# First modulation in four quarters of two feature tiles, x and ctx loaded first, key products placed beside the gate and value products

## What is computed

```python
sh_a, sc_a, g_a, sh_f, sc_f, g_f = jnp.split(
    (jax.nn.silu(c) @ w_ada[l] + b_ada[l])[:, None, :], 6, axis=-1)
...
hc = modulate(rmsnorm(ctx, norm_mix[l]), csh_a, csc_a)
hx = modulate(rmsnorm(x, norm_mix[l]), sh_a, sc_a)
...
u = h @ w_in
```

## Time and profile before

| | us |
|---|---|
| median of three runs | 1447.3 |
| the profiled run, device time | 1446.77 |
| its span, first to last instruction | 1444.9 |
| outside the span | 1.87 |
| PE busy in the span | 1395.9 (97%) |
| PE's waits for modulation chunks in the first 110 us | 14.9 |
| first product of `first_linear` | 31.30 |
| first product of ka | 46.95 |
| first product of qa | 52.46 |
| first scores of the attention | 75.40 |

### The profile page before, as it was taken

How to read it: one execution, slowest core, us unless ns; L and a number is a source line. 1 busy time by engine, 2 the same in 40 slices (tenths; PEclk the granted TensorE clock), 3 DMA queues, 4 the chain that set the end, 5 groups by cost and what they waited for, 6 DMA issues and landing times.

```text
span 1444.9 us, 21620 instructions
## 1 busy us (share of the span) xinstructions
PE 1395.9 (97%) x8272; PEld 1165.5 (81%) x8272; DVE 848.0 (59%) x1638; ACT 657.8 (46%) x1069; POOL 839.9 (58%) x672
## 2 busy tenths in 40 slices
PE   5999999999999999889999999999999999999998
PEld 3977798999988889547788888888888966888887
DVE  3798666786568798687664333321136667644422
ACT  3555755455553234783332222222226386545443
POOL 1534427999855444785254554544446630799997
PEclk9999999999999999999999999999999999999999
DMA  9748515777767753001355555533333320455664
GB/s 365 292 162 303 177 46 195 254 259 233 259 230 247 237 180 98 27 30 59 131 204 188 190 201 189 191 108 97 104 95 115 118 77 12 135 187 190 187 189 135
DMA packets 71207, 242.01 MB, mean 167 GB/s; under 512 B 7488, under 2 KB 12992, under 8 KB 70720
## 3 DMA queue, kind: packets, MB, share of 16 engines
q1 hardware_dynamic: 68688, 236.63, 49.2%
q10 hardware_dynamic: 2416, 4.00, 0.9%
HBM read 238.50 MB, written 1.05 MB: 166 GB/s over the span
## 4 chain that ended last, share of the span: by engine, by line
PE 51%; DVE 4%; ACT 2%; issue 1%; POOL 0%; DMA 0%; DVEq 0%; ACTq 0%
PE bank L762 9%; PE bank L768 9%; PE bank L763 9%; PE bank L623 8%; PE bank L624 4%; PE bank L614 1%; PE bank L616 1%; PE bank L615 1%; PE cond_a L1160 1%; PE bank L622 1%; PE bank L1160 1%; DVE h_both L2282 1%; PE bank L1168 1%; PE cond_a L1221 1%; PE bank L1180 1%
## 5 line engine op out<-in xcount | busy, mean ns | idle before, releaser
L2050 POOL TENSOR_TENSOR w_lo<-raw,w_hi 128x512 fp32r<-128x512 f32 (+2 forms) x610 | 776.4, 1302 | 575.0 <-ACT w_hi L1502 566.3
L1502 ACT ACTIVATE w_hi<-raw 128x1024 fp32r<-128x1024 f32 (+3 forms) x300 | 308.2, 1030 | 589.5 <-PE bank L768 352.8
L762 PE MATMUL bank<-h_both,w_hi 128*128 128x512 f32 (+1 forms) x1000 | 321.1, 340 | 0.4 <-ACT w_hi L1502 0.3
L763 PE MATMUL bank<-h_both,w_hi 128*128 128x512 f32 (+1 forms) x1000 | 320.2, 339 | 0.0
L762 PEld LDWEIGHTS bank<-h_both,w_hi 128*128 128x128 f32 x1000 | 188.0, 188 | 22.4 <-issue 0.5
L763 PEld LDWEIGHTS bank<-h_both,w_hi 128*128 128x128 f32 x1000 | 188.0, 188 | 21.3
L768 PE MATMUL bank<-h_both,w_lo 128*128 128x512 f32 (+1 forms) x1000 | 198.1, 339 | 0.4 <-POOL w_lo L2050 0.2
L768 PEld LDWEIGHTS bank<-h_both,w_lo 128*128 128x128 f32 x1000 | 159.6, 188 | 22.6 <-POOL w_lo L2050 1.4
L2164 DVE CUSTOM_DVE_ANT_0 ada_junk<-ada_w,cond_a 128x1024 bf16<-128x1024 f32 x128 | 153.9, 1216 | 12.3 <-DVE work L2733 8.1
L2146 DVE TENSOR_TENSOR hidden_both<-work,hidden_both 128x256 fp32r<-128x256 f32 (+1 forms) x66 | 58.6, 888 | 142.7 <-ACT hidden_both L1587 142.7
L623 PE MATMUL bank<-h_both,w_hi 128*128 128x512 f32 x345 | 123.1, 394 | 0.8 <-POOL w_lo L2050 0.8
(11 more groups left out here) (487 smaller groups left out, 2507.9 us busy)
## 6 DMA issues: line engine op xcount, KB each, us to landing
raw<-in_up SPq DMA_DIRECT2D x132, 512.0 KB, 3.6
ada_w<-in_ada SPq DMA_DIRECT2D x128, 512.0 KB, 4.5
raw<-in_down SPq DMA_DIRECT2D x48, 448.0 KB, 3.5
raw<-in_out SPq DMA_DIRECT2D x24, 512.0 KB, 3.6
raw<-in_down SPq DMA_DIRECT2D x24, 512.0 KB, 3.6
raw<-in_in SPq DMA_DIRECT2D x24, 512.0 KB, 5.0
arena<-in_ada SPq DMA_DIRECT2D x16, 512.0 KB, 11.7
raw<-in_uq SPq DMA_DIRECT2D x12, 384.0 KB, 3.0
```

Of the source, the lines that this page charges most:

```text
L762: pe.matmul(out, w_h[:, k - k0], hi[:, k, cols], start=(k == 0), stop=False)
L763: pe.matmul(out, w_h[:, k - k0], lo[:, k, cols], start=False, stop=False)
L1502: act.activation(part_slot(w_hi, f, u), raw_slot(f, u), ACT.Copy).then_inc(s["rounded"], 1)
L2050: pool.tensor_tensor(part_slot(w_lo, f, u)[:, a:b], raw_slot(f, u)[:, a:b], part_slot(w_hi, f, u)[:, a:b].bitcast(F32), ALU.subtract).then ...
```

## The change

The modulation comes in four quarters of two feature tiles. The chunks are laid out anew, so that four of them hold a quarter (shift and scale of tiles 2j and 2j+1). `ada_quarter(j)` takes four chunks with eight products of 128 columns each. SP loads x, ctx and the fixed table ahead of the first four chunks, then the weights of va_gates and of ka, then the other twelve chunks, then two units of qa, and only then the table and the conditioning rows. `first_linear` makes the key products of each tile beside its gate and value products, in a third bank; the phase for ka is gone. Quarters 1, 2 and 3 stand behind the products of tiles 0, 2 and 4, and their columns between the key products and the value products of tiles 1, 3 and 5. ACT rounds the ka unit before the norm's shifts, and the first qa unit once tile 3's value products are done (`va_part`). DVE takes the first rows ahead of the norm, and from tile 2 on the order is lower(k-1), rows, modulation, scaled(k) at each even k. `gate_sums` and `gate_rows` follow query units 1 and 3.

```diff
             sp.dma_start(cond_t, dram["cond_t"].rearrange("p (k m) -> p k m", k=KD)).then_inc(s["cond_t_in"], 16)
-            load_first_ada(0, 3)
             sp.dma_start(X[:, :, L0:L1], dram["x"]).then_inc(s["x_in"], 16)
             sp.dma_start(X[:, :, 0:L0], dram["ctx"]).then_inc(s["x_in"], 16)
             sp.dma_start(fixed[:, :], dram["table3"]).then_inc(s["fixed_in"], 16)
-            load_first_ada(3, 8)
+            load_first_ada(0, 4)
...
-                    if g == 1:
-                        load_first_ada(8, 16)
                     if g == 2:
+                        load_first_ada(4, 16)
+                    if g == 4:
...
-            def ada_chunk(q):
-
-                pe.wait_ge(first_ada_in[q], 16)
-                k = q % KD
-                for g in range(4):
-                    last = pe.matmul(bank[3 + q // KD][32 * g:32 * g + 32, 0:LAT], cond_t[:, k, :],
-                                     first_ada[:, q, g * LAT:(g + 1) * LAT], start=(k == 0), stop=(k == KD - 1))
-                if k == KD - 1:
-                    last.then_inc(s["ada_half"], 1)
-
-            def ada_columns(half):
-
-                pe.wait_ge(s["ada_rows"], half + 1)
+            def ada_quarter(j):
+
+                for q in range(4 * j, 4 * j + 4):
+                    pe.wait_ge(first_ada_in[q], 16)
+                    for e in range(2):
+                        k = q % 4 * 2 + e
+                        for g in range(4):
+                            last = pe.matmul(bank[3 + j % 2][32 * g:32 * g + 32, j // 2 * P:(j // 2 + 1) * P],
+                                             cond_t[:, k, :], first_ada[:, q, (4 * e + g) * P:(4 * e + g + 1) * P],
+                                             start=(k == 0), stop=(k == KD - 1))
+                last.then_inc(s["ada_part"], 1)
+
+            def ada_columns(j):
+
+                pe.wait_ge(s["ada_rows"], j + 1)
                 picked = ident.rearrange("p (g c) -> p g c", g=4)[:, :, 0:2]
-                out = bank[6][:, 16 * half:16 * half + 16].rearrange("p (g j m) -> p j g m", g=4, j=2)
-                for j in range(2):
-                    last = pe.matmul(out[:, j], ada_rows[:, half, j * P:(j + 1) * P], picked, start=True, stop=True)
-                last.then_inc(s["ada_cols"], 1)
+                out = bank[6][:, 8 * j:8 * j + 8].rearrange("p (g m) -> p g m", g=4)
+                pe.matmul(out, ada_rows[:, j, :], picked, start=True, stop=True).then_inc(s["ada_cols"], 1)
 
             def first_linear(gate):
+
                 _, h_hi, h_lo = features("va_gates")
-
-                f = ph["va_gates"]
-                chunks = {0: (8, 9, 10, 11), 2: (12, 13, 14, 15)}
-                for k in range(KD):
-                    for q in chunks.get(k, ()):
-                        ada_chunk(q)
-                    if k == 2:
-                        ada_columns(1)
+                f, g = ph["va_gates"], ph["ka"]
+
+                def values(k):
                     u, n = divmod(k, KD // 2)
                     if n == 0:
                         pe.wait_ge(s["split"], 2 * (f.first_unit + u + 1))
                     w_h, w_l = (part_slot(x, f, u)[:, n * 144:n * 144 + 256] for x in (w_hi, w_lo))
-                    gate(k)
                     for i in range(TT):
                         last = three(bank[i // 2][:, i % 2 * 256:i % 2 * 256 + 256], h_hi[:, k, i * P:(i + 1) * P],
                                      h_lo[:, k, i * P:(i + 1) * P], w_h, w_l, k == 0 and i % 2 == 0,
                                      k == KD - 1 and i % 2 == 1)
                         if k == KD - 1 and i % 2:
                             last.then_inc(s["steps"], 1)
+                    if k == KD // 2 - 1:
+                        last.then_inc(s["va_part"], 1)
+
+                def keys(k):
+                    if k == 0:
+                        pe.wait_ge(s["split"], 2 * (g.first_unit + 1))
+                        room(g.first_taken)
+                    w_h, w_l = (part_slot(x, g, 0, KD)[:, k] for x in (w_hi, w_lo))
+                    last = three(bank_of(g.first_taken)[:, :], w_h, w_l, h_hi[:, k, :], h_lo[:, k, :], k == 0, k == KD - 1)
+                    if k == KD - 1:
+                        last.then_inc(s["steps"], 1)
+
+                for k in range(KD):
+                    gate(k)
+                    if k % 2 and k + 1 < KD:
+                        keys(k)
+                        ada_columns((k + 1) // 2)
+                        values(k)
+                    else:
+                        values(k)
+                        keys(k)
+                        if k + 2 < KD:
+                            ada_quarter(k // 2 + 1)
...
-            for q in range(KD):
-                ada_chunk(q)
+            ada_quarter(0)
             pe.wait_ge(s["fixed_in"], 16)
+            ada_columns(0)
             token_sums(0, TOK)
-            ada_columns(0)
             spread_inverse(0, TOK)
             first_linear(next_h())
-            linear("ka", 0, TOK)
 
             def rows_of_gates(u):
 
-                if u == 0:
+                if u == 1:
                     pe.wait_ge(s["tables_in"], 16)
                     gate_sums()
-                if u == 2:
+                if u == 3:
...
+                    if (f0.name, u0) == ("va_gates", 0):
+                        act.wait_ge(s["va_part"], 1)
+                    else:
+                        act.wait_ge(s["steps"], f0.steps_after(u0))
...
             rms_std(0, TOK)
+            round_next()
             round_next()
             round_next()
...
-            def first_rows(half):
-
-                dve.wait_ge(s["ada_half"], half + 1)
-                copy(ada_rows[:, half, :], bank[3 + half][:, 0:LAT]).then_inc(s["ada_rows"], 1)
-
-            def first_modulation(half):
-
-                dve.wait_ge(s["ada_cols"], half + 1)
-                m = mod[:, 0, 0:16, :].rearrange("p (s f) m -> p s f m", s=2)[:, :, 4 * half:4 * half + 4, :]
-                b = S("b_ada0")[:, 0:16].rearrange("p (s f) -> p s f", s=2)[:, :, 4 * half:4 * half + 4]
-                shift, scale = (bank[6][:, 16 * half + 8 * i:16 * half + 8 * i + 8].rearrange("p (f m) -> p f m", f=4)
+            def first_rows(j):
+
+                dve.wait_ge(s["ada_part"], j + 1)
+                copy(ada_rows[:, j, :], bank[3 + j % 2][:, j // 2 * P:(j // 2 + 1) * P]).then_inc(s["ada_rows"], 1)
...
-                    first_rows(0)
+                    first_modulation(0)
                 else:
                     round_third(third)
                 invert(0 if both else L0, L1, joint)
-                if first:
-                    first_modulation(0)
...
-                    if first and k == KD // 2:
+                    part = first and k % 2 == 0
+                    if part:
                         lower(k - 1)
-                        first_rows(1)
-                        first_modulation(1)
+                        first_rows(k // 2)
+                        first_modulation(k // 2)
                     scaled(k)
-                    if not first or k != KD // 2:
+                    if not part:
...
             add_squares(0, TOK)
+            first_rows(0)
             norm(0, True, True)
```

23 lines of the change are left out of this document (14 added, 9 removed).

## The result

The changed kernel takes 1461.1 us (median of four runs, 1459.71 to 1463.56); the kernel before took 1447.6 on the same chip. The ratio is 1.0097, with a 95% interval of 1.0084 to 1.0111: slower by 14 us, where the prediction said 8. The profiled execution took 1460.91 us, with a span of 1459.1, against 1446.77 and 1444.9. It lies outside the forecast's own range of 1453 to 1458: the size is wrong by 6 us.

The account below looks back on a forecast made before the run. PE, busy 97% of the span, was taken as the bound. A 4.1 us earlier norm, PE 6.7 late at the queries and gates 9.6 late, less a 1.19 wait, left 8.4: 1446.77 + 8.4 = 1455.2 us, range 1448.5 to 1461.5.

Parts of the forecast that it names:

- Step 1: Loads and norm: x and ctx behind three fewer chunks, first scaled tile at 24.15 instead of 28.24, a 4.1 us gain.
- Rival (e): Start: the norm does not start earlier, as x and ctx fill no time better; 4.1 us more, 1459.3; chance 0.05.
- Step 2: First tile: its rest is there 2.89 us after scaled starts, at 27.0 against 31.30.
- the third rounding: ACT at the norm: rounding ahead of the shifts ends at 24.0, first shift due at 25.0, so it costs nothing.
- Step 3: Quarters on PE's path: three now stand between products, making PE 6.7 us late at the queries.
- The ring: Tiles: DVE's scaled awaits columns, PE reaches these behind tile, keys and quarter, then waits; 8.6 us between columns, three times.
- rival (b): Quarters: half-width products miss the wide ones' pace, a quarter takes 3.9 instead of 1.93; 5.8 us more, 1461; chance 0.10.
- Step 4: Gates: softplus loses the keys' cover, DVE's gate chain starts 9.6 us late, scores 8.4 late at 83.8.
- (a): Behind the gates: DVE's lateness is made good further on, only PE's own counts; 1452.4 us; chance 0.20.
- (d): Within noise: clock rises at once, DVE's delay doesn't count, downstream load waits give back two more; 1448.8 us; chance 0.10.
- (c): Tiles: quarters and keys fall into PE's waits and DVE's chain sets the pace; faster, 1443.2 us; chance 0.08.
- The tests: Signs that would refute the forecast: first query product before 53, or scores less than 5 us late.

Follow-up runs that it names:

- e12_x_late: Changed kernel with three chunks of the modulation loaded ahead of x and ctx again; 1467.2 us, ratio 1.0138.
- e3_late_round: Changed kernel with ACT's rounding of the key unit moved from ahead of its first shift to behind its second; 1460.6 us, ratio 1.0108.
- e1_fill_ring: Changed kernel with four junk products of 256 columns on PE ahead of tiles 2, 4 and 6; 1459.0 us, ratio 1.0094.
- e6_before_keys_beside: Kernel before with key products beside each tile's gates and values, gates' sums and rows one query unit later, modulation still in halves; 1453.1 us, ratio 1.0032.
- e10_before_pe_delay: Kernel before with 27 junk products of 256 columns on PE between the last value product and the first key product; 1459.8 us, ratio 1.0091.
- e5_earlier: Changed kernel with each quarter one pair of tiles earlier and the columns behind the even tile's values, ahead of its keys; 1449.5 us, ratio 1.0020.
- e11_improved: e5_earlier with each tile's keys behind the next tile's values, softplus ahead of ACT's second qa rounding, key unit rounded behind the second shift; 1446.1 us, ratio 0.9993.
- e4_keys_apart: Changed kernel with the key products in a loop of their own behind the values of all eight tiles; 1460.6 us, ratio 1.0112.
- e8_earlier_keys_late: e5_earlier with the keys of tiles 4 to 7 behind the values of the last tile; 1448.7 us, ratio 1.0007.

## What held in the prediction, and the step that failed

**Step 1** holds, and more: squares at 11.15 (said 11.8), root at 20.94 (21.4), `scaled(0)` at 23.56 (24.15), a gain of 4.7 us instead of 4.1. Rival (e) is refuted, and e12_x_late shows that the gain reaches the end.

**Step 2** has a mis-sized term. The rest of tile 0 was put at 2.89 from a tile of before; it took 28.34 - 23.56 = 4.78, and without POOL's split beside it 2.79 (e3_late_round). I had costed the third rounding at nothing, "under" ACT's spare time, and looked at ACT alone. What it set off on POOL was the cost. Less the 0.6 us by which step 1 did better than its sum, the first value product is 1.3 us late.

**Step 3** has the step that failed. The ring, its three waits and its parts are right: waits of 1.89 (said 2.2), a quarter in 1.95 (1.93; rival (b) is refuted), and 8.70 us a turn wherever the clock stayed up (8.6). But I asked only when the clock would first rise and gave bounds for that alone. I didn't ask what each of the three waits that I had just predicted would do to it. It fell behind every one and cost 4.6 us (30.05 from the first columns to the queries, 25.4 in e1_fill_ring, where the clock stayed up, and 25.2 in my sum). So this term, which I had put at nothing, is the larger part of the miss. Tile 0's lateness, of which 1.1 us is left at the first columns, the 4.6, and 0.2 in small terms are the 6.0 us between 59.2 and 65.17. The Trainium skill ("TensorE: Matmul & The Clock Gate", section "HAM oscillation — how this bites in real kernels") describes this pattern, a loop that waits and then starts each turn at the low level; the three windows at 0.57 agree. The waits in its example are longer than the 1.89 us here, so the page did not foretell these falls, but it raises the question that I left out, and I used that page for rival (b) only.

**Step 4** has the right mechanism as far as the softplus goes: it ended last, at 68.93, and e6_before_keys_beside shows the lost cover by itself. It is not the larger part, though. The sum left out that DVE copies the keys ahead of `log_gates`, so that PE's lateness reaches the gate chain by this way also (e10_before_pe_delay). It changes no figure of the sum, because the softplus is the later of the two. The 9.6 us of DVE's lateness became 15.7; all but 0.1 of this growth comes from steps 2 and 3. From there to the scores the sum allowed for 1.19 us less than before, since a load wait goes. It does go, but DVE's rotations pay for part of that beside POOL. First the kernel after, then before, between 52 and 92 us:

```profile
L3140 DVE TENSOR_TENSOR arena<-arena 128x256 f32<-128x256 f32 x2 | 3.0, 1500 | 0.0
...
L3141 DVE TENSOR_TENSOR arena<-arena 128x256 f32<-128x256 f32 x2 | 2.8, 1400 | 0.1
```

```profile
L3121 DVE TENSOR_TENSOR arena<-arena 128x256 f32<-128x256 f32 x2 | 1.9, 968 | 0.0
...
L3122 DVE TENSOR_TENSOR arena<-arena 128x256 f32<-128x256 f32 x2 | 0.9, 426 | 0.1
```

That is 5.8 us instead of 2.8. Other operations ran beside a split before and don't now: `log_gates` to the first rotation takes 2.92 us instead of 4.15, and one operation of the last rotation (128x768) 0.96 instead of 1.96. From `log_gates` to the scores it is 21.6 us, where the sum had 20.9 and before 22.1, so the scores are 6.8 us later than forecast and not 6.1. The later stages give 1.0 back, which leaves the profiled execution at 1460.9 against my 1455.2.

**The rivals.** (a) and (d) are too fast. (b) names the measured time, 1461, by luck: its quarter of 3.9 us took 1.95. (c) needed PE's turn under 5.4 us; it was 10.2. The case that came true, the forecast's own mechanism with the clock lost in every turn, was not among them. It should have been one: bounds for its price could be had from rows, V and K at half pace against full pace (4.2 against 2.1), for none to all of the three waits. **The tests** that I named were passed in the main (queries after 53, scores more than 5 us late), but they asked only for too little.

## What to carry to other kernels

When a sum predicts that PE will idle in a loop, price the work behind each idle stretch at both clock levels; left out, it was 4.6 us here, beside a forecast loss of 8.4. When work is moved ahead on one engine because that engine has time, look at what it releases on the next one. And a product that only prepares a later tile belongs ahead of the wait, not between a tile and the columns that release the next: with the same three quarters the scores came 15.2 us late in one order (after) and within 0.6 us of the kernel before in two others (e5_earlier, e11_improved). When a delay is put in to part two causes, check in the trace that the second cause stayed where it was; here a copy of the keys tied the two together.

## What the runs showed of the hardware

An idle stretch of PE of 1.89 us was enough for the granted clock to fall, behind three of three in after, two of three in e3_late_round, one of three in e4_keys_apart, and also behind the one in e8_earlier_keys_late (granted clock 0.58) and the three in e12_x_late (0.63 to 0.64). It fell behind none in e1_fill_ring, where junk products filled it. In after the fall shows within half a microsecond of PE's return: products of 256 columns 0.12 us apart at 1.00 stand 0.21 apart.

DVE operations with both tensors in SBUF took three times as long beside POOL's splits (0.48 to 1.48 us for `h_both`, 0.43 to 1.50 for the rotations), while `scaled`, which reads one of its operands from a bank of PSUM, keeps its 477 ns in the same microseconds. The Trainium skill ("GPSIMD Engine Reference", section "1. Specifications") says that GpSimd contends with DVE instructions that have two SBUF inputs; the trace agrees, with these numbers.
